# Even mixer: each pooling product behind the first unit of the next quad, the last one inside the out projection's first quad

## What is computed

```python
def multiscale_pool(u, pool_w, pool_scale):
    ...
    p = jnp.stack(groups, axis=2).astype(u.dtype)
    y = jnp.einsum('bsgc,gcd->bsgd', p, pool_w).reshape(bsz, s, B_W)
    return y * pool_scale

def even_mixer(h, w_in, conv_w, pool_w, pool_scale, w_out):
    z = h @ w_in
    gate_b = z[..., :A_W]
    gate_c = z[..., A_W:2 * A_W]
    val = z[..., 2 * A_W:3 * A_W]
    pool_in = z[..., 3 * A_W:]
    y_a = gate_b * causal_dwconv(gate_c * val, conv_w)
    y_b = multiscale_pool(pool_in, pool_w, pool_scale)
    return jnp.concatenate([y_a, y_b], axis=-1) @ w_out
```

## Time and profile before

| | us |
|---|---|
| median of 3 runs | 996.73 |
| the three runs | 996.92, 994.44, 996.73 |
| span of the profiled execution, first to last instruction | 994.4 |
| PE busy in it | 936.8 (94%) |
| DVE busy in it | 648.7 (65%) |

### The profile page before, as it was taken

The page is one execution under the profiler, slowest core; times in us unless marked ns, Lnnn a source line. Parts: engine busy times, 40 slices in busy tenths (PEclk is TensorE's granted clock), DMA queues, the critical chain, the costliest instruction groups (busy, mean ns, idle before and its releaser), DMA issues.

```text
span 994.4 us, 20944 instructions
## 1 busy us (share of the span) xinstructions
PE 936.8 (94%) x7618; PEld 912.8 (92%) x7618; DVE 648.7 (65%) x1109; ACT 526.3 (53%) x847; POOL 376.2 (38%) x158
## 2 busy tenths in 40 slices
PE   8899999994699899999999999989999999999994
PEld 8789999994699899999999999979899999999993
DVE  6998766660454855576666564789747877765366
ACT  6346755550444455575555554545557766664353
POOL 3333434440442432234433433313322444343452
PEclk9899999998799999999999999989999999999997
DMA  7445666572643344456555654334333655565521
GB/s 259 158 148 174 206 201 199 188 232 75 200 166 107 132 151 135 136 173 213 185 172 195 226 184 154 107 127 139 117 121 133 201 188 182 173 228 186 179 80 43
DMA packets 46173, 163.37 MB, mean 164 GB/s; under 512 B 4985, under 2 KB 9593, under 8 KB 46123
## 3 DMA queue, kind: packets, MB, share of 16 engines
q1 hardware_dynamic: 41704, 158.19, 48.7%
q10 hardware_dynamic: 4419, 4.49, 1.3%
HBM read 161.58 MB, written 3.31 MB: 166 GB/s over the span
## 4 chain that ended last, share of the span: by engine, by line
PE 55%; issue 21%; DVE 12%; POOL 5%; ACT 3%; another core or an unknown queue 3%; DMA 1%; SPq 0%; POOLq 0%; ACTq 0%; DVEq 0%
PE psum L1239 17%; PE psum L1240 17%; PE psum L1241 17%; POOL wl L434 5%; DVE work L878 2%; DVE wl L781 1%; DVE h L1214 1%; ACT wh L479 1%; DMA raw<-in_even_in 1%; PE psum L1411 1%; ACT work L640 1%; PE psum L1380 1%; DVE work L1072 1%; PE psum L1388 1%
## 5 line engine op out<-in xcount | busy, mean ns | idle before, releaser
L434 POOL TENSOR_TENSOR wl<-raw,wh 128x1024 fp32r<-128x1024 f32 (+2 forms) x137 | 358.8, 2620 | 581.1 <-ACT wh L479 580.9
L1239 PE MATMUL psum<-xs,wh 128*128 128x256 f32 x1632 | 467.9, 287 | 4.3 <-DVE xs L797 2.1
L1240 PE MATMUL psum<-xs,wh 128*128 128x256 f32 x1632 | 463.2, 284 | 0.0
L1241 PE MATMUL psum<-xs,wl 128*128 128x256 f32 x1632 | 463.1, 284 | 0.0
L479 ACT ACTIVATE wh<-raw 128x1024 fp32r<-128x1024 f32 (+2 forms) x270 | 300.8, 1119 | 286.0 <-PE psum L1241 250.9
L1239 PEld LDWEIGHTS psum<-xs,wh 128*128 128x128 f32 x1632 | 314.5, 193 | 10.9 <-issue 4.0
L1240 PEld LDWEIGHTS psum<-xs,wh 128*128 128x128 f32 x1632 | 314.6, 193 | 0.2
L1241 PEld LDWEIGHTS psum<-xs,wl 128*128 128x128 f32 x1632 | 314.4, 193 | 0.0
L781 DVE TENSOR_TENSOR wl<-raw,wh 128x1024 fp32r<-128x1024 f32 (+1 forms) x133 | 183.8, 1382 | 125.1 <-ACT wh L479 125.0
L1239 PE MATMUL psum<-ys,wh 128*128 128x256 f32 x672 | 192.5, 286 | 22.1 <-DVE h L946 22.1
L1240 PE MATMUL psum<-ys,wh 128*128 128x256 f32 x672 | 191.3, 285 | 0.0
(11 more groups left out here) (195 smaller groups left out, 726.5 us busy)
## 6 DMA issues: line engine op xcount, KB each, us to landing
raw<-in_up SPq DMA_DIRECT2D x132, 512.0 KB, 4.1
raw<-in_down SPq DMA_DIRECT2D x48, 704.0 KB, 4.4
raw<-in_qkv SPq DMA_DIRECT2D x48, 512.0 KB, 3.3
raw<-in_even_in SPq DMA_DIRECT2D x16, 512.0 KB, 4.3
raw<-in_out SPq DMA_DIRECT2D x16, 512.0 KB, 3.4
raw<-in_ple SPq DMA_DIRECT2D x8, 640.0 KB, 3.8
raw<-in_even_out SPq DMA_DIRECT2D x8, 512.0 KB, 3.2
toeplitz_dram<-table_dram ACTq DMA_DIRECT2D x1, 2176.0 KB
```

Of the source, the lines that this page charges most:

```text
L434: nc.gpsimd.tensor_tensor(low, raw[:, s, 0:tiles * P], high.bitcast(f32), ALU.subtract)\
L1239: nc.tensor.matmul(bank, high_w[:, w], high, start=first, stop=False)
L1240: nc.tensor.matmul(bank, high_w[:, w], low, start=False, stop=False)
L1241: done = nc.tensor.matmul(bank, low_w[:, w], high, start=False, stop=last)
```

## The change

It moves instructions and renumbers the chunks of `ys`; the work is the same.

- On PE `pool_product(j)` stands behind unit 0 of quad j + 1 for all j. The last, of group 3, stands in the out projection behind tiles 0 to 5 of unit 0. The tables stand behind unit 1 of quad 2.
- The out projection's first quad does tiles 0 to 5 of all four units, and then tiles 6 and 7 of all four.
- On DVE the pooled low part of group j stands in quad j + 1, behind `even_p`. That of group 3 stands behind the split of slot 3 of quad 4.
- On ACT the high part of the convolution's chunk comes first and the pooled one behind it.
- Chunk 2j of `ys` is now the convolution's and 2j + 1 the pooled one, and the rows of the out weights are ordered to match.

```diff
@@ act
                 for s in range(1 if j == 0 else 0, RING):
                     round_ahead("even_in", j, s)
+                act.wait_ge(even_ready, j + 1)
+                round_ys(2 * j, even_y)
                 act.wait_ge(pooled, j + 1)
-                round_ys(2 * j, aux[:, 0, 0:SEQ], scale=column("pool_scale", j), func=ACT.Identity)
-                act.wait_ge(even_ready, j + 1)
-                round_ys(2 * j + 1, even_y)
+                round_ys(2 * j + 1, aux[:, 0, 0:SEQ], scale=column("pool_scale", j), func=ACT.Identity)
@@ dve
+            def low_pooled(j):
+                dve.wait_ge(yh_ready, 2 * j + 2)
+                nc.vector.scalar_tensor_tensor(ys[:, 2 * j + 1, 1, :], aux[:, 0, 0:SEQ], column("pool_scale", j),
+                                               ys[:, 2 * j + 1, 0, :].bitcast(f32), ALU.mult, ALU.subtract).then_inc(ys_ready, 1)
...
                 split_ahead("even_in", j, 0)
+                if j >= 1:
+                    low_pooled(j - 1)
                 scaled(even_c, 1, j).then_inc(bank_read, 1)
...
-                dve.wait_ge(yh_ready, 2 * j + 1)
-                nc.vector.scalar_tensor_tensor(ys[:, 2 * j, 1, :], aux[:, 0, 0:SEQ], column("pool_scale", j),
-                                               ys[:, 2 * j, 0, :].bitcast(f32), ALU.mult, ALU.subtract).then_inc(ys_ready, 1)
-                low_ys(2 * j + 1, even_y, "even_in", 2 * j + 1)
+                low_ys(2 * j, even_y, "even_in", 2 * j)
                 if j == quads_of["even_in"] - 1:
                     split_ahead("even_in", j, 3)
+                    low_pooled(j)
@@ pe
                 if j == 0:
                     pe.wait_ge(pool_landed, 2 * 16)
                 else:
-                    pe.wait_ge(ys_ready, 2 * j - 1)
+                    pe.wait_ge(ys_ready, 2 * j)
...
-                    if j == 1 and s == 0:
-                        pool_product(0)
-                if j >= 1:
-                    pool_product(j)
-                if j == 1:
-                    tables()
+                    if j >= 1 and s == 0:
+                        pool_product(j - 1)
+                    if j == 2 and s == 1:
+                        tables()
             q = base["even_out"]
 
-            begin(q, (0, 1), slot_bank, lambda s: slot_read(q, s), from_ys, lambda t: pe.wait_ge(ys_ready, t + 1), late=2)
-            quad_of("even_out", from_ys)(0, (2, 3))
+
+            for s in range(RING):
+                unit(q, s, slot_bank(s), from_ys, range(DC - 2), stop=False,
+                     ready=(lambda t: pe.wait_ge(ys_ready, t + 1)) if s == 0 else None, read=slot_read(q, s))
+                if s == 0:
+                    pool_product(quads_of["even_in"] - 1)
+            for s in range(RING):
+                unit(q, s, slot_bank(s), from_ys, range(DC - 2, DC), start=False,
+                     ready=(lambda t: pe.wait_ge(ys_ready, t + 1)) if s == 0 else None).then_inc(units_done, 1)
```

More of the change, by code:

```diff
@@ L1607 @@
     arrays["even_in"] = weight_units(a["ev_w_in"][0], even_order)
-    pool_first = np.arange(D).reshape(2, D // 2 // P, P)[::-1].transpose(1, 0, 2).reshape(-1)
-    arrays["even_out"] = weight_units(a["ev_w_out"][0][pool_first], natural)
+    by_turns = np.arange(D).reshape(2, D // 2 // P, P).transpose(1, 0, 2).reshape(-1)
+    arrays["even_out"] = weight_units(a["ev_w_out"][0][by_turns], natural)
     for layer, (w_up, w_down) in enumerate(((a["ffn_w_in"][0], a["ffn_w_out"][0]), (a["ffn_w_in"][1], a["ffn_w_out"][1]),
```

## The result

The changed kernel takes 998.76 us (median of 11 runs, 997.69 to 999.86), the kernel before 996.73 (11 runs, 994.44 to 997.97). The ratio is 1.0025, with a 95% interval of 1.0016 to 1.0034: slower by 2.0 us in the medians and 2.5 by the ratio.

The account below looks back on a forecast made before the run. It took PE's waits to decide the whole kernel, with DVE never free in the even in projection. DVE's -1.46 was already inside PE's net +1.8, which on the median of 996.73 gave 998.5 us, range 995.0 to 1002.0.

Parts of the forecast that it names:

- DVE's one wait goes, 1.46 us: Even in projection: DVE's wait for PE before quad 2's first bank vanishes; slot 3's split in quad 4 ends at 73.92.
- the 1.5 allowed: First four quads: DVE instructions held up by POOL's splits were taken as 0 net change, with 1.5 us either side.
- Unit 0 ends with the split, ACT rounds at 77.13: Out projection's first quad: unit 0 must wait for slot 3's split, so ACT rounds quad 5's slot 0 2.1 us later.
- PE waits for POOL at 80.75 and for chunk 7 at 96.7, by 2.2 us: PE waits 1.7 us for POOL before quad 5, then some 2.2 for the residual's chunk 7 in quad 6.
- Statistics at 100.3: Quad 6: PE's statistics come at 100.3 instead of 98.51, 1.8 us later.
- the first rival, the clock: New PE gaps near 65 to 68, 79 and 94.5 drop the clock: 2.9 us more, +4.7 in all, 1001.4; chance 0.24.
- a clock of 0.50 behind 65 us: Sign that the prediction is wrong: PE's granted clock at the 1.2 GHz level anywhere behind 65 us.
- Nothing behind quad 6 changes, and PE runs from there with its work queued, so the 1.8 stays.: From quad 6 to the end: PE carries its 1.8 us lateness through, 994.4 becoming 996.2 for the profiled execution.
- The pass-through of PE's stops, 7.7 us: Rival with PE as the bound: stops of 2.62 and 2.20 and 2.9 of clock go, giving 989; chance 2 in 100.
- A faster kernel by shed stalls: Rival: earlier POOL splits free DVE of some of 13.7 us of stall; three shed give -4.8, 991.9; faster has 0.11.
- The prediction's rule: Shared DVE and POOL ports lock for a whole instruction: a DVE instruction meeting a split pays its rest, 0 to 2.4 us.

Follow-up runs that it names:

- the late-issue run: Kernel before, with only ACT's issue of the 2176 KB transfer to toeplitz_dram moved from behind the out projection's residual to behind the norm's root: 999.23 us against 996.87.

## Why the prediction was right, and where it was not

The number holds: 998.5 forecast, 998.76 measured. The steps in the out projection hold too; the step from there to the end of the kernel does not, and that the number is right all the same is luck. One by one:

- *DVE's one wait goes, 1.46 us.* Right. The split of slot 3 was put at 73.92 and ends at 73.14. Of the 0.78 between, 0.36 is the program's earlier start (first statistics at 18.25 against 18.61); the rest is what DVE's stretched instructions, which the prediction counts as POOL's stalls, came to, inside the 1.5 allowed.
- *Unit 0 ends with the split, ACT rounds at 77.13.* Right: 76.42, which is 3.28 us behind the end of the split where the working had 3.21. The lateness against the trace of before is 1.4, not 2.1, since the split came earlier.
- *PE waits for POOL at 80.75 and for chunk 7 at 96.7, by 2.2 us.* Right: 79.98, 95.90 and 1.99.
- *Statistics at 100.3.* 101.09, 2.6 later than before, not 1.8. From chunk 7's tile to the statistics the 30 matmuls took 101.09 - 95.90 = 5.2 us instead of 3.6, at 1.2 GHz from 97 to 100 us. That is the first rival, the clock, at 1.6 us instead of 2.9; half of it is hidden by chunk 7, which came 0.8 earlier than forecast. The prediction named a clock of 0.50 behind 65 us as a sign that it is wrong, and this sign came. Its argument against the rival, that the clock had not fallen behind the stop of 2.20 us, was one trace's luck: behind the same stop the late-issue run has 0.58.
- *"Nothing behind quad 6 changes, and PE runs from there with its work queued, so the 1.8 stays."* This step failed. PE does run through to 236 us, and its 2.6 us come that far undiminished, but then it stands for 22.1 us in the down projection (21.85 in the changed kernel), until a transfer has landed. The page's slices show it (PE at 4 tenths in one and 6 in the next), and the prediction read waits only up to 105 us. What carried the change to the end is the transfer that ACT issues behind the residual chain, 1.3 us later, and the weight loads that run 2.0 us longer beside it: its landing is 2.3 later. That the landing gives +2.0 in the medians and the wrong step +1.8 is chance; with the measured 2.6 at the statistics the wrong step would have said 999.3. By the estimate from the two rates, a kernel that had delayed PE without delaying the chain would have been charged only 0.45 of it; no run shows that case.
- *The pass-through of PE's stops, 7.7 us.* Rightly given 2 in 100: the first stop and the half clock behind it went, the second moved by three matmuls, and nothing was gained.
- *A faster kernel by shed stalls.* Did not come. The stretched time moved from some instructions to others: the ten sums take 14.1 us instead of 15.8 and the four TENSOR_SCALAR (L896, now L903) 1.4 instead of 3.6, but the eight splits take 11.2 instead of 9.7, the corrections (L884, now L889) 2.8 instead of 1.5, and the pooling inputs (L887, now L892) 2.5 instead of 1.7.

What stays open: how the 2.0 us of the timed runs divide between the issue (by the estimate 0.55 x 1.32 = 0.7) and the later pause of the loads (0.45 x 2.0 = 0.9). No run delayed one alone with the other fixed; the late issue moved both.

## What to carry to other kernels

A pause that is removed from the busiest engine is worth nothing if its partner in the pipeline was the one that had no time; ask which instruction the *next* stage starts with, and do not put it behind the last thing that the slow engine makes. Here, ending four units together put the end of the first behind a late split and 18 matmuls more, and DVE lost there more (2.63 us) than the wait that was removed (1.46). And before a lateness is carried to the end of a kernel, look for the next long stop of the bounding engine: if there is one, what feeds that stop is what counts, even if it was issued 140 us earlier, as here (95.3 for a stop from 235.9 on).

## What the runs showed of the hardware

A transfer DRAM to DRAM of 17 x 128 rows of 1 KB used 1.1 engines' worth of 16 when alone and took 155 us. Its 9 rows by themselves used 9.4 engines' worth in 98 to 102 us, and with 9 and 8 rows issued one behind the other all of it was through within 30 us. The Trainium skill, "DMA: Bandwidth & Descriptors", section "Why a DMA increments its semaphore by 16 and not by 1", says that a transfer goes to as many engines, up to 16, as the largest number that divides the slowest dimension (of those larger than 1) of both its access patterns. By that rule 17 rows give one engine and 9 rows give nine, and the trace agrees, with 1.1 and 9.4. No run here tried 16 rows.

The transfer on one engine fell from 24 GB/s alone to 13.2 GB/s beside the weight loads.

Whether a short stop of PE costs the clock is not settled by its length. Behind the stop of 2.20 us in front of the product of group 3 the granted clock was 1.00 in the trace of before and 0.58 (70 to 74 us) in the late-issue run, with the same code up to there; behind the stop of 2.28 us in front of tile 5 it was 1.00 in the changed kernel and 0.55 (68 to 71 us) with the out projection's order undone.

Which DVE instructions POOL's splits hold up shows in the changed kernel, POOL's split of a slot and the three DVE instructions that meet it:

```profile
48.33 2.68 POOL L434 TENSOR_TENSOR wl<-raw,wh 128x1024 fp32r<-128x1024 f32 x1 [1.00 <-ACT wh L479]
```

```profile
48.66 0.48 DVE L875 SCALAR_TENSOR_TENSOR ys<-psum,vec,ys 128x256 fp32r<-128x256 f32 x1
49.06 0.41 DVE L820 TENSOR_TENSOR work<-psum,rstd 128x256 f32<-128x256 f32 x1
49.39 2.71 DVE L781 TENSOR_TENSOR wl<-raw,wh 128x1024 fp32r<-128x1024 f32 x1
```

The first two read one operand from PSUM and take their usual 0.48 and 0.41 us inside the split. The third reads both from SBUF and takes 2.71 instead of 1.21: it ends 1.1 us behind POOL's, as if it had done nearly all its work after it. The prediction's rule, that a DVE instruction which meets a split pays the rest of it, is so too wide: the two that read PSUM paid nothing.
